# Banded attention inside a chunked delta rule: one masking pass, normalising on ScalarE, and the transpose of the weights behind the chunk's products

## The chip, the cores and the metric

The kernel runs on one core of a Trainium2 chip. The time is device microseconds of one execution. The core has TensorE (PE; its weight loads are shown as PEld), VectorE (DVE), ScalarE (ACT), GpSimd (POOL) and SyncE (SP), each with its own instruction queue, executed in order. They wait for each other only by semaphores.

## The reference

Two layers follow one another in float32 on 512 tokens of width 1024. The first mixes a gated delta rule (4 heads of 128, in chunks) with a dilated attention (8 heads of 64), adds a gated feed-forward network, and the second block holds a gated recurrence of 16 heads and a Fourier mixer. The change touches the dilated attention only:

```python
DIL_PATTERNS = ((128, 1), (512, 4), (2048, 16))
# each (window, dilation) branch attends to t, t-d, ..., t-window
s = einsum(q * Dh**-0.5, k); s = where(valid, s, -inf); m = max(s)
p = exp(s - m); den = sum(p); num = p @ v
# the three branches are merged by exp(m_i - m_all)
out = num_tot / den_tot
```

A key that several branches see counts as often as branches see it. So the three branches together are one softmax over keys 0 to t in which the exponential of each key is multiplied by a count from 0 to 3.

## The kernel before

**The stage.** After the input projections (tiles 0 to 27) come four chunks c = 0 to 3 of 128 tokens of the delta rule. In each, the inverse of a triangular 128 x 128 matrix per head is built up in six levels l = 1 to 6, all four heads side by side in one 512 wide operation. A level is a chain over three engines:

- TensorE: T = xx by mask product (L663, into bank 3), semaphore T.
- ScalarE: copies it to `tt` (L1101), semaphore Te.
- TensorE: XA (L673, bank 4; not in level 6) and XX (L676, bank 5).
- VectorE: subtracts them from `xx` (L1504) and `xt` (L1506). T of the next level needs `xx` and the next mask product (L1498).

Ahead of the levels is the chunk's head: VectorE forms decay differences (L1462, L1464), ScalarE takes exponentials (L1092 to L1094, semaphore eex), VectorE forms `ee` (L1470), `lt`, `at_`, the first `xt` (L1481), after which TensorE transposes it (L649). Behind the levels (step 7) TensorE forms two products (L682, L684), ScalarE copies both (L1105, L1106, semaphore uwe), TensorE forms the product with the state (L690), VectorE subtracts it (L1512), and TensorE forms output and state update (L696 to L701).

**The attention.** Its 32 blocks n (head n // 4, query block n % 4, (n % 4 + 1) * 128 keys) are woven into these steps, one per step, n = 8c + l with l = 0 to 7. Each block goes through:

- `scores(n)` on TensorE (L581, bank 0);
- `front(n)` on VectorE: scale and mask (L1420), maximum (L1423), its negative (L1425);
- `weights(n)` on ScalarE: exponential in place in `sm` (L1065);
- `back(n)` on VectorE: times the counts, with their sum (L1433, an instruction and a read of its accumulator), reciprocal (L1436), normalise (L1438, semaphore p_ready);
- `turn(n)` on TensorE: transposes the weights into bank 1 (L593), one per 128 keys;
- `place(n)` on ScalarE: copies them to `pT` (L1072);
- per head, `weigh(h)` on TensorE: weights by values (L602, bank 2); per pair of heads `pair_high` (ScalarE, L1084) and `pair_low` (VectorE, L1442) take the result out.

`sm` and `pr` have two buffers, banks 0, 1 and 2 one each.

**Order.** All queues are written out by hand in the program's order; no planner is involved. In step n VectorE does back(n-1), front(n), then the level's work. ScalarE copies T, then place(n-1), then weights(n). `attention_tail(n)` on TensorE is weigh of the head before, where n % 4 is 1, then turn(n-1); in a level it stands between T and the wait for Te. `scores(n+1)` follows XX. In ScalarE's `attention_tail(n)`, pair_high comes first for n = 9, 17, 25.

**Beside it.** In the same steps GpSimd multiplies streamed modulation weights (L424, L428, L432, two buffers in `mod`), and TensorE adds them up (`modulation`, L453) behind T, up to 1.3 sums per step. SyncE loads these weights.

Of the kernel before, what the change touches and what calls it, by code (L numbers as in the profile page):

```python
# [18 lines left out]
ALU = mybir.AluOpType  # L19
ACT = mybir.ActivationFunctionType  # L20
AX = mybir.AxisListType

P = 128
# [135 lines left out]
def build(nc, d, out, upto=99, debug=None):  # L159
# [4 lines left out]
    with ctx:  # L164
        sems = {}

        def S(name):
            if name not in sems:
                sems[name] = ctx.enter_context(nc.semaphore("s_" + name))
            return sems[name]  # L170
# [268 lines left out]
        def _(pe):  # L439
# [136 lines left out]
            def scores(n):  # L576
                h, i = n // 4, n % 4
                o = 64 * (h % 2)
                if n:
                    pe.wait_ge(S("sm_ready"), n)  # L580
                pe.matmul(bank[0][:, 0:(i + 1) * P], bqkv[o:o + 64, h // 2, i * P:(i + 1) * P],  # L581
                          bqkv[o:o + 64, 4 + h // 2, 0:(i + 1) * P], start=True, stop=True).then_inc(S("s_done"), 1)
# [30 lines left out]
            def attention_tail(n):  # L613
                if n >= 1:
                    if n % 4 == 1 and n > 1:
                        weigh(n // 4 - 1)
                    turn(n - 1)
# [3 lines left out]
            for c in range(TT):  # L621
                tok = slice(c * P, (c + 1) * P)
                n = 8 * c
                pe.wait_ge(S("ug"), c + 1)
                for h in range(4):
                    mm = pe.matmul(bank[3][:, h * P:(h + 1) * P], ones[:], G["ug"][:, h, :], start=True, stop=True)
                mm.then_inc(S("gr"), 1)
                if c:
                    pe.wait_ge(S("o_ev"), c)
                    pe.wait_ge(S("st_upd"), c)  # L630
                else:
                    pe.wait_ge(S("l2_rs"), 8)
                    pe.wait_ge(S("l2_done"), 8)
                for h in range(4):
                    pe.matmul(bank[4][:, h * P:(h + 1) * P], qkv[:, 4 + h, tok], qkv[:, 4 + h, tok], start=True, stop=True)
                for h in range(4):
                    pe.matmul(bank[5][:, h * P:(h + 1) * P], qkv[:, 4 + h, tok], qkv[:, h, tok], start=True, stop=True)
                for h in range(4):
                    mm = pe.transpose(bank[6][:, h * P:(h + 1) * P], qkv[:, 8 + h, tok], ident[:])
                mm.then_inc(S("kk"), 1)  # L640
                attention_tail(n)

                pe.wait_ge(S("eex"), c + 1)
                for h in range(4):
                    mm = pe.transpose(bank[3][:, h * P:(h + 1) * P], qkv[:, 4 + h, tok], ident[:])
                mm.then_inc(S("vk"), 1)
                pe.wait_ge(S("x1"), c + 1)
                for h in range(4):
                    mm = pe.transpose(bank[4][:, h * P:(h + 1) * P], G["xt"][:, h, :], ident[:])  # L649
                mm.then_inc(S("x1T"), 1)  # L650
                scores(n + 1)
                modulation(n)
                for l in range(1, 7):
                    q = 6 * c + l
                    n = 8 * c + l
                    pe.wait_ge(S("m_rdy"), q)
                    if l == 1:
                        pe.wait_ge(S("x1e"), c + 1)
                        pe.wait_ge(S("gkv"), c + 1)
                    else:  # L660
                        pe.wait_ge(S("xx_upd"), 5 * c + l - 1)
                    for h in range(4):
                        mm = pe.matmul(bank[3][:, h * P:(h + 1) * P], G["m%d" % (l % 2)][:, h, :], G["xx"][:, h, :],  # L663
                                       start=True, stop=True)
                    mm.then_inc(S("T"), 1)
                    modulation(n)
                    attention_tail(n)
                    pe.wait_ge(S("Te"), q)
                    if l > 1:
                        pe.wait_ge(S("x_upd"), q - 1)  # L670
                    if l < 6:
                        for h in range(4):
                            mm = pe.matmul(bank[4][:, h * P:(h + 1) * P], G["xt"][:, h, :], G["tt"][:, h, :], start=True, stop=True)  # L673
                        mm.then_inc(S("XA"), 1)
                    for h in range(4):
                        mm = pe.matmul(bank[5][:, h * P:(h + 1) * P], G["tt"][:, h, :], G["xt"][:, h, :], start=True, stop=True)  # L676
                    mm.then_inc(S("XX"), 1)
                    scores(n + 1)
                n = 8 * c + 7
                pe.wait_ge(S("x_upd"), 6 * c + 6)  # L680
                for h in range(4):
                    pe.matmul(bank[6][:, h * P:(h + 1) * P], G["xt"][:, h, :], G["vtok"][:, h, :], start=True, stop=True)  # L682
                for h in range(4):
                    mm = pe.matmul(bank[5][:, h * P:(h + 1) * P], G["gk"][:, h, :], G["xt"][:, h, :], start=True, stop=True)  # L684
                mm.then_inc(S("uw"), 1)
                attention_tail(n)
                pe.wait_ge(S("uwe"), c + 1)
                if c:
                    for h in range(4):
                        mm = pe.matmul(bank[3][:, h * P:(h + 1) * P], G["wkT"][:, h, :], G["st"][:, h, :], start=True, stop=True)  # L690
                    mm.then_inc(S("PS"), 1)
                pe.wait_ge(S("u"), c + 1)
                for h in range(4):
                    o = bank[4][:, h * P:(h + 1) * P]
                    if c:
                        pe.matmul(o, G["st"][:, h, :], G["qdec"][:, h, :], start=True, stop=False)  # L696
                    mm = pe.matmul(o, G["u"][:, h, :], G["at_"][:, h, :], start=(c == 0), stop=True)
                mm.then_inc(S("o"), 1)
                if c < TT - 1:
                    for h in range(4):  # L700
                        mm = pe.matmul(bank[5][:, h * P:(h + 1) * P], G["kend"][:, h, :], G["u"][:, h, :], start=True, stop=True)  # L701
                    mm.then_inc(S("ds"), 1)
                if c < TT - 1:
                    scores(n + 1)
                modulation(n)
# [210 lines left out]
        def _(act):  # L916
# [144 lines left out]

            def weights(n):
                w = (n % 4 + 1) * P
                act.wait_ge(S("nmx_ready"), n + 1)
                do(A.activation(sm[:, n % 2, 0:w], sm[:, n % 2, 0:w], ACT.Exp, bias=nmx[:, n:n + 1]), "pexp")  # L1065

            def place(n):
                h, i = n // 4, n % 4
# [6 lines left out]
            def attention_tail(n):  # L1075
                if n > 8 and n % 8 == 1:
                    pair_high(n // 8 - 1)
                if n:
                    place(n - 1)

            def pair_high(hp):
# [208 lines left out]
        def _(dve):  # L1290
# [123 lines left out]
            def front(n):  # L1414

                w = (n % 4 + 1) * P
                dve.wait_ge(S("s_done"), n + 1)
                if n >= 2:
                    dve.wait_ge(S("p_ready"), n - 1)
                do(X.scalar_tensor_tensor(sm[:, n % 2, 0:w], bank[0][:, 0:w], 0.125, dneg[:, T - w:T],  # L1420
                                          ALU.mult, ALU.add), "sm_ready")
                do.settle()
                do(X.tensor_reduce(mx[:, n:n + 1], sm[:, n % 2, 0:w], AX.X, ALU.max))  # L1423
                do.settle()
                do(X.tensor_scalar(nmx[:, n:n + 1], mx[:, n:n + 1], -1.0, None, ALU.mult), "nmx_ready")  # L1425

            def back(n):

                w = (n % 4 + 1) * P
                dve.wait_ge(S("pexp"), n + 1)  # L1430
                if n >= 2:
                    dve.wait_ge(S("pT_done"), n - 1)
                do(X.tensor_tensor_reduce(pr[:, n % 2, 0:w], sm[:, n % 2, 0:w], dcnt[:, T - w:T], 1.0, 0.0, ALU.mult, ALU.add,  # L1433
                                          den[:, n:n + 1]))
                do.settle()
                do(X.reciprocal(rden[:, n:n + 1], den[:, n:n + 1]))  # L1436
                do.settle()
                do(X.tensor_scalar(pr[:, n % 2, 0:w], pr[:, n % 2, 0:w], rden[:, n:n + 1], None, ALU.mult), "p_ready")  # L1438

            def pair_low(hp):  # L1440
                dve.wait_ge(S("ob_hi"), hp + 1)
# [2 lines left out]
            def attention_tail(n):  # L1444
                if n:
                    back(n - 1)
                if n > 8 and n % 8 == 2:
                    pair_low(n // 8 - 1)
# [375 lines left out]
```

## Time and profile before

| | us |
|---|---|
| median of three runs | 2395.82 (2393.82 to 2396.49) |
| the profiled execution, its own time | 2398.15 |
| its span, first to last instruction | 2396.4 |
| TensorE busy (share) | 2229.8 (93%) |
| VectorE busy | 1456.6 (61%) |
| ScalarE busy | 708.6 (30%) |
| GpSimd busy | 284.4 (12%) |
| mean granted TensorE clock | 0.958 of full speed |

Busy times are sums over the whole span, so they hide that stages differ: in the stretch of the four chunks (215 to 462 us) TensorE is busy for 201.69 of 247 us, VectorE for 185.06, GpSimd for 156.42, ScalarE for 58.84, with a granted clock of 0.88. In the timelines an instruction's start and its duration stand in microseconds; where an engine had been idle before it, brackets say how long and what ended the wait. Durations of TensorE products overlap, so distances between starts tell more than durations. The granted clock of a stretch is a mean: 1.00 is 2.4 GHz throughout, 0.50 would be 1.2 GHz throughout.

### The profile page before, as it was taken

To read this page: it belongs to the slowest core of one execution; us is meant where nothing else is said; L and a number is where in the kernel's file an instruction comes from. 1 tells how busy PE (TensorE), PEld (TensorE's weight loads), DVE (VectorE), ACT (ScalarE), POOL (GpSimd) and SP (SyncE) were. 2 spreads that over 40 slices of the span, in tenths; PEclk is the share of its full clock that TensorE was granted. 3 is DMA by queue.
4 is the path that set the end of the run, shared out by engine and by line. 5 is a ranking of instruction groups with operands and counts; after the bars stand their busy time and mean duration, and the time that the engine had idled before them with its cause. 6 is when DMAs were issued, how large, how long until landed. Compare 5 with 4: busy or idle time off the path is not lost.

```text
span 2396.4 us, 27171 instructions
## 1 busy us (share of the span) xinstructions
PE 2229.8 (93%) x10851; PEld 1781.4 (74%) x10851; DVE 1456.6 (61%) x2253; ACT 708.6 (30%) x1111; POOL 284.4 (12%) x196
## 2 busy tenths in 40 slices
PE   6998888789999997999999999999998898999998
PEld 4876666567888885788887877787886486888886
DVE  5634678638758583577777777777777624333332
ACT  4363222434324334222222222222221223332332
POOL 0011766423233120000000000000000000000000
PEclk9998888999999998999999999999999599999999
DMA  4331111233434332111111111111111022223221
GB/s 142 97 83 36 44 45 53 80 106 107 122 114 136 110 117 77 53 45 52 46 44 48 50 45 53 45 44 53 45 45 44 0 79 88 67 71 88 62 62 44
DMA packets 311134, 164.31 MB, mean 69 GB/s; under 512 B 6268, under 2 KB 308194, under 8 KB 311010
## 3 DMA queue, kind: packets, MB, share of 16 engines
q1 hardware_dynamic: 311010, 162.59, 23.2%
q8 instruction: 87, 1.43, 0.2%
q14 instruction: 37, 0.30, 0.0%
HBM read 160.47 MB, written 2.10 MB: 68 GB/s over the span
## 4 chain that ended last, share of the span: by engine, by line
PE 73%; DVE 18%; issue 4%; ACT 3%; POOL 0%; SPq 0%; DMA 0%; ACTq 0%; DVEq 0%; POOLq 0%
PE bank L470 16%; PE bank L472 16%; PE bank L471 16%; DVE KC L1673 3%; DVE MT L1695 3%; DVE QC L1675 2%; DVE QQ L1680 2%; PE bank L815 2%; PE bank L505 2%; PE bank L489 1%; PE bank L487 1%; PE bank L488 1%; PE bank L887 1%; PE bank L851 1%; PE bank L876 1%
## 5 line engine op out<-in xcount | busy, mean ns | idle before, releaser
L1307 DVE TENSOR_TENSOR wl<-stage,wh 128x1024 fp32r<-128x1024 f32 (+1 forms) x248 | 310.7, 1254 | 670.8 <-ACT wh L929 670.7
L470 PE MATMUL bank<-hh,wh 128*128 128x512 f32 x1536 | 642.5, 418 | 32.6 <-DVE hl L1325 17.7
L472 PE MATMUL bank<-hh,wl 128*128 128x512 f32 x1536 | 606.5, 395 | 0.0
L471 PE MATMUL bank<-hl,wh 128*128 128x512 f32 x1536 | 605.6, 394 | 0.0
L929 ACT ACTIVATE wh<-stage 128x1024 fp32r<-128x1024 f32 (+1 forms) x248 | 260.1, 1050 | 1034.1 <-PE bank L472 613.1
L470 PEld LDWEIGHTS bank<-hh,wh 128*128 128x128 f32 x1536 | 292.5, 190 | 110.2 <-issue 40.8
L472 PEld LDWEIGHTS bank<-hh,wl 128*128 128x128 f32 x1536 | 292.1, 190 | 63.9
L471 PEld LDWEIGHTS bank<-hl,wh 128*128 128x128 f32 x1536 | 293.6, 191 | 59.0 <-issue 5.7
L470 PE MATMUL bank<-gh,wh 128*128 128x512 f32 x432 | 179.0, 414 | 10.9 <-DVE gl L1536 6.6
L424 POOL TENSOR_TENSOR mprod<-stage,gs 128x1024 f32<-128x1024 f32 x64 | 130.8, 2043 | 463.7 <-DMA stage<-in_ada_w 458.8
L471 PE MATMUL bank<-gl,wh 128*128 128x512 f32 x432 | 170.0, 393 | 0.0
L472 PE MATMUL bank<-gh,wl 128*128 128x512 f32 x432 | 169.9, 393 | 0.0
L794 PE MATMUL bank<-QC,KC 128*128 128x128 f32 x1024 | 141.2, 283 | 7.5 <-DVE MT L1695 7.5
L794 PEld LDWEIGHTS bank<-QC,KC 128*128 128x128 f32 x1024 | 135.7, 199 | 14.9 <-issue 9.0
L487 PE MATMUL bank<-ch,wh 128*128 128x256 f32 x384 | 112.4, 293 | 0.0
L488 PE MATMUL bank<-cl,wh 128*128 128x256 f32 x384 | 108.7, 283 | 0.0
L489 PE MATMUL bank<-ch,wl 128*128 128x256 f32 x384 | 108.7, 283 | 0.0
L470 PEld LDWEIGHTS bank<-gh,wh 128*128 128x128 f32 x432 | 82.0, 190 | 33.5 <-DVE gl L1536 7.0
L1673 DVE TENSOR_TENSOR KC<-KK,QQ 128x512 f32<-128x512 f32 x144 | 101.0, 702 | 6.2 <-PE bank L794 5.2
L1675 DVE TENSOR_TENSOR QC<-qs,PP 128x512 f32<-128x512 f32 x144 | 100.7, 700 | 0.0
L428 POOL TENSOR_TENSOR mprod<-mprod 128x512 f32<-128x512 f32 x64 | 99.7, 1558 | 5.0
L1688 DVE TENSOR_TENSOR PP<-PP 128x512 f32<-128x512 f32 x144 | 97.7, 679 | 0.6
(295 smaller groups left out, 2974.1 us busy)
## 6 DMA issues: line engine op xcount, KB each, us to landing
stage<-in_hg_w_in SPq DMA_DIRECT2D x80, 512.0 KB, 3.6
stage<-in_ada_w SPq DMA_DIRECT2D x48, 512.0 KB, 3.6
stage<-in_w_up SPq DMA_DIRECT2D x44, 512.0 KB, 3.8
stage<-in_ft_w_in SPq DMA_DIRECT2D x32, 512.0 KB, 3.9
stage<-in_w_in SPq DMA_DIRECT2D x28, 512.0 KB, 3.8
stage<-in_w_down SPq DMA_DIRECT2D x16, 512.0 KB, 4.0
stage<-in_hg_w_out SPq DMA_DIRECT2D x16, 512.0 KB, 3.9
stage<-in_ft_w_out SPq DMA_DIRECT2D x16, 512.0 KB, 3.9
```

The source lines that it names most:

```text
L424: do(nc.gpsimd.tensor_tensor(mprod[:], stage[:, u["slot"], :, :], view(silc[:, v:v + 1], [[2, KT], [0, P]]), ALU.mult), f"stage_free{u['sl ...
L470: pe.matmul(bank[t % NLIN][:], wh[:, s, k, :], xh[:, k, :], start=a, stop=False)
L471: pe.matmul(bank[t % NLIN][:], wh[:, s, k, :], xl[:, k, :], start=False, stop=False)
L472: mm = pe.matmul(bank[t % NLIN][:], wl[:, s, k, :], xh[:, k, :], start=False, stop=b)
L487: pe.matmul(o, wh[:, s, k, :], ch[:, k, :], start=a, stop=False)
L488: pe.matmul(o, wh[:, s, k, :], cl[:, k, :], start=False, stop=False)
L489: mm = pe.matmul(o, wl[:, s, k, :], ch[:, k, :], start=False, stop=b)
L794: mm = pe.matmul(b[:, a * P:(a + 1) * P], kc[:, a * P:(a + 1) * P], qc[:, a * P:(a + 1) * P], start=True, stop=True)
L929: do(A.activation(wh[:, l % NSPLIT, 0:nk, :], stage[:, u["slot"], 0:nk, :], ACT.Copy), "hi_ready")
L1307: do(X.tensor_tensor(wl[:, l % NSPLIT, 0:nk, :], stage[:, u["slot"], 0:nk, :], wh[:, l % NSPLIT, 0:nk, :].bitcast(F32), ALU.subtract), f"s ...
L1673: do(X.tensor_tensor(view(kc[:, 0:1], flat), view(KK[:, 0, 0:1], sel), view(QQ[:, 0, 0:1], sel), ALU.mult))
L1675: do(X.tensor_tensor(view(qc[:, 0:1], flat), view(q[:, 0:1], flat), view(PP[:, 0, 0:1], [[2 * n, nb], [n - T, 2], [1, n]], T), ALU.mult), ...
```

## The change

Mask, scale and maximum become one VectorE instruction with an accumulator: it adds the mask to the unscaled scores, multiplies by -0.125 and takes the minimum, which is the negative of the maximum. `sm` holds the negated scaled scores, and the exponential has scale -1. Normalising moves from VectorE's L1438 to a ScalarE copy with a scale per partition, placed ahead of place(n-1). The reciprocal now signals `rden_ready`. In levels 1 to 6, TensorE's `attention_tail(n)` moves from between T and the wait for Te to behind XX, ahead of scores(n+1). Steps 0 and 7 keep TensorE's order.

```diff
@@ TensorE, levels 1 to 6
                     mm.then_inc(S("T"), 1)
                     modulation(n)
-                    attention_tail(n)
                     pe.wait_ge(S("Te"), q)
...
                     mm.then_inc(S("XX"), 1)
+                    attention_tail(n)
                     scores(n + 1)
@@ ScalarE
             def weights(n):
                 w = (n % 4 + 1) * P
-                act.wait_ge(S("nmx_ready"), n + 1)
-                do(A.activation(sm[:, n % 2, 0:w], sm[:, n % 2, 0:w], ACT.Exp, bias=nmx[:, n:n + 1]), "pexp")
+                act.wait_ge(S("sm_ready"), n + 1)
+                do(A.activation(sm[:, n % 2, 0:w], sm[:, n % 2, 0:w], ACT.Exp, scale=-1.0, bias=nmx[:, n:n + 1]), "pexp")
+
+            def normalise(n):
+                w = (n % 4 + 1) * P
+                act.wait_ge(S("rden_ready"), n + 1)
+                do(A.activation(pr[:, n % 2, 0:w], pr[:, n % 2, 0:w], ACT.Copy, scale=rden[:, n:n + 1]), "p_ready")
...
                 if n > 8 and n % 8 == 1:
                     pair_high(n // 8 - 1)
                 if n:
+                    normalise(n - 1)
                     place(n - 1)
@@ VectorE, front(n)
                 if n >= 2:
-                    dve.wait_ge(S("p_ready"), n - 1)
-                do(X.scalar_tensor_tensor(sm[:, n % 2, 0:w], bank[0][:, 0:w], 0.125, dneg[:, T - w:T],
-                                          ALU.mult, ALU.add), "sm_ready")
-                do.settle()
-                do(X.tensor_reduce(mx[:, n:n + 1], sm[:, n % 2, 0:w], AX.X, ALU.max))
-                do.settle()
-                do(X.tensor_scalar(nmx[:, n:n + 1], mx[:, n:n + 1], -1.0, None, ALU.mult), "nmx_ready")
+                    dve.wait_ge(S("rden_ready"), n - 1)
+
+                do(X.tensor_tensor_reduce(sm[:, n % 2, 0:w], bank[0][:, 0:w], dneg[:, T - w:T], -0.125, 3e38, ALU.add, ALU.min,
+                                          nmx[:, n:n + 1]), "sm_ready")
@@ VectorE, back(n)
                 do.settle()
-                do(X.reciprocal(rden[:, n:n + 1], den[:, n:n + 1]))
-                do.settle()
-                do(X.tensor_scalar(pr[:, n % 2, 0:w], pr[:, n % 2, 0:w], rden[:, n:n + 1], None, ALU.mult), "p_ready")
+                do(X.reciprocal(rden[:, n:n + 1], den[:, n:n + 1]), "rden_ready")
```

## Rows read from the trace of the kernel before

**Rows 1.** The page's part 4: the last chain by engine.

```profile
PE 73%; DVE 18%; issue 4%; ACT 3%; POOL 0%; SPq 0%; DMA 0%; ACTq 0%; DVEq 0%; POOLq 0%
```

**Rows 2.** Windows: stretch, length, busy by engine, clock; level 1, then levels 2-6.

```profile
284.84:295.94 11.10, 11.10 (x43) 7.63 (x44) 4.13 (x12) 1.76 (x4) 7.77 (x6) 0.62 0.16 47
...
233.00:262.79 29.79, 27.16 (x168) 21.95 (x167) 21.87 (x49) 7.53 (x15) 23.22 (x16) 0.89 0.15 43
295.94:325.02 29.08, 26.09 (x167) 20.08 (x166) 22.48 (x50) 7.76 (x15) 24.63 (x19) 0.94 0.19 55
359.34:386.59 27.25, 24.50 (x168) 19.51 (x167) 24.58 (x50) 7.75 (x15) 24.86 (x18) 1.00 0.20 59
422.92:452.64 29.72, 26.27 (x171) 21.28 (x170) 26.46 (x50) 7.72 (x15) 21.10 (x15) 0.94 0.33 98
```

**Rows 3.** Groups by shape, 215 to 462 us: busy us, mean ns, idle before.

```profile
L1433 DVE CUSTOM_DVE_ANT_0 pr<-sm,dcnt 128x512 f32<-128x512 f32 x8 | 7.9, 988 | 0.0
L1065 ACT ACTIVATE sm<-sm,gs 128x512 f32<-128x512 f32 x8 | 5.8, 723 | 1.1 <-DVE gs L1425 1.0
L1420 DVE SCALAR_TENSOR_TENSOR sm<-bank,dneg 128x512 f32<-128x512 f32 x8 | 5.4, 680 | 0.0
L1065 ACT ACTIVATE sm<-sm,gs 128x384 f32<-128x384 f32 x8 | 4.9, 615 | 3.1 <-DVE gs L1425 3.0
L1433 DVE DVE_READ_ACCUMULATOR2_ANT gs<- 128x1 f32 x32 | 2.5, 78 | 0.0
```

**Rows 4.** Timeline of VectorE, head of the third chunk: start, duration.

```profile
341.89 0.17 DVE L1436 RECIPROCAL gs<-gs 128x1 f32<-128x1 f32 x1
...
343.18 0.28 DVE L1420 SCALAR_TENSOR_TENSOR sm<-bank,dneg 128x128 f32<-128x128 f32 x1
...
343.89 1.13 DVE L1470 SCALAR_TENSOR_TENSOR g_ee<-g_ee,gs,cst 128x128 f32<-128x128 f32 x4
```

**Rows 5.** Timeline of TensorE and ScalarE in levels 4 to 6, second chunk.

```profile
308.69 1.06 PE L673 MATMUL bank<-g_tt,g_xt 128*128 128x128 f32 x8
309.58 1.06 PE L676 MATMUL bank<-g_xt,g_tt 128*128 128x128 f32 x8
...
320.12 0.91 PE L581 MATMUL bank<-bqkv 64*128 64x384 f32 x2
320.96 1.16 PE L663 MATMUL bank<-g_xx,g_m 128*128 128x128 f32 x8
322.16 0.60 ACT L1101 ACTIVATE g_tt<-bank 128x512 f32<-128x512 f32 x1 [3.04 <-PE bank L663]
322.71 0.44 PE L593 MATMUL bank<-ident,pr 128*128 128x128 f32 x2 [0.59 <-DVE pr L1438]
322.99 1.06 PE L676 MATMUL bank<-g_xt,g_tt 128*128 128x128 f32 x8
323.97 1.12 PE L581 MATMUL bank<-bqkv 64*128 64x512 f32 x2
325.02 1.16 PE L682 MATMUL bank<-g_vtok,g_xt 128*128 128x128 f32 x8
```

**Rows 6.** Timeline of ScalarE: the pair copy in level 1 of the second chunk.

```profile
292.91 0.60 ACT L1084 ACTIVATE gh<-bank 128x512 fp32r<-128x512 f32 x1 [5.36 <-PE bank L602]
```

**Rows 7.** Timeline of TensorE: second chunk's state product, and the stage's end.

```profile
328.25 1.16 PE L690 MATMUL bank<-g_st,g_wkT 128*128 128x128 f32 x8 [0.68 <-ACT g_wkT L1106]
...
459.76 0.60 PE L593 MATMUL bank<-ident,pr 128*128 128x128 f32 x4
461.10 2.37 PE L602 MATMUL bank<-pT,bqkv 128*64 128x512 f32 x8 [0.74 <-ACT pT L1072]
```

**Rows 8.** Timelines of TensorE and GpSimd: modulation sums, chunks 1, 3 and 4.

```profile
245.96 1.01 PE L453 MATMUL bank<-ones,mod 128*128 128x1 f32 x4 [1.53 <-POOL mod L432]
...
366.00 1.20 PE L453 MATMUL bank<-ones,mod 128*128 128x1 f32 x8
...
440.75 0.72 POOL L432 TENSOR_TENSOR mod<-mprod 128x256 f32<-128x256 f32 x1
```

## The prediction, made before the changed kernel was run

> **What bounds the kernel now.** I read the page's parts 1 and 4 first, then the windows of the stage that the diff touches, then the timelines of single levels. Over the whole span the chain that ended last is 73% TensorE and 18% VectorE [rows 1]; most of that TensorE share is dense projections the diff never enters. The diff lives between 215 and 462 us: four chunks of the gated delta rule, with 32 attention blocks (n = 0 to 31, eight per chunk, key width 128 to 512) woven in, so at most about a tenth of the time can move. Inside it I need to know, level by level, which wait ends last.
>
> Levels 2 to 6 of the four chunks last 29.79, 29.08, 27.25 and 29.72 us, with VectorE busy 22 to 26 us of each and TensorE 24 to 27 [rows 2]. Neither is full: they take turns. Call T the products at L663, XA those at L673, XX those at L676. T ends, ScalarE copies it (0.60 us), and XX or XA may start: 320.96 to 322.76, so 1.83 us from T's start with the hop. In this row block's turn (L593) was queued ahead and held XX to 322.99, 0.59 us of it TensorE waiting for VectorE's normalised weights [rows 5]. That is the wait the change is aimed at. In others T itself waited for VectorE's update of xx, which sits behind back, front and the next mask product on VectorE.
>
> **What goes.** Per block VectorE loses L1438, L1423 and L1425, and L1420 becomes a two-instruction reduction (the form of L1433: a main pass and an accumulator read of 0.08 us) [rows 3]. The new pass with a PSUM source is not in the trace. Below: 0.68 us at width 512, what L1420 takes; above: 0.99 us, the mean of L1433, whose two SBUF sources are sometimes stretched [rows 3]. I take 0.68, because one source stays in PSUM as in L1420. That removes about 1 to 1.4 us of VectorE per block, some 35 us in all, but only the part that ends a wait counts.
>
> (1) Chunk heads. Here VectorE alone is the path: back(8c-1) and front(8c) stand between the decay differences and L1470. In the third chunk the reciprocal ends at 342.06 and L1470 starts at 343.89. With front(128) alone between them (0.28 + 0.08) it starts at 342.44: 1.45 us less [rows 4]. The fourth chunk repeats this. In the second the normalise was short, I count 0.9. The first has no back and waits for ScalarE's exponentials anyway: 0. Sum -3.8 us. After L1470 everything hangs on VectorE, so nothing takes this back at once.
>
> (2) Levels 2 to 6. With VectorE lighter I rebuild a level from TensorE's own order: T to XA 1.83; XA to XX 0.90; XX to the next product 0.98; scores 0.84 for three key blocks and 1.05 for four, so 0.21 per block and 0.42, 0.63 for one and two; turn 0.28 for two blocks, 0.14 per block [rows 5]; the weighted values (L602) 2.3 [rows 7]. Turn now lies behind XX and thus in series. Level 2: 3.71 + 0.28 + 1.05 = 5.04. Level 3: 3.71 + 0.42 + 0.42 = 4.55. Level 4: 3.71 + 0.56 + 0.63 = 4.90. Level 5: 3.71 + 2.3 + 0.14 + 0.84 = 6.99. Level 6, without XA: 1.83 + 0.98 + 0.28 + 1.05 = 4.14. Together 25.6 us, 1.6 to 4.2 below the windows, 13.4 us over four chunks. That is the best end of this term.
> But two things in those windows are not VectorE's. One is GpSimd: TensorE executes modulation sums behind T, and waited 1.53 us for one in the first chunk (level 4); in the third the sums of level 3 ended at 367.20 [rows 8], 0.85 us later than the rebuilt level would want XA. In the fourth the second sum of level 5 is ready at 441.47; with 0.4 us of its products XA starts at 441.9, and the rebuilt level would have reached it at 422.92 + 1.03 (below) + 14.49 + 1.83 = 440.3, so 1.6 us wait. The second chunk has a wait like the first's, of about 0.9. The other is the clock: a granted 0.89, 0.94, 1.00, 0.94 [rows 2] means that 22%, 12%, 0 and 12% of the windows ran at 1.2 GHz, and the products lost 3.3, 1.7, 0 and 1.8 us by it. I keep both, since the idle spots that caused it (GpSimd waits) stay. New windows: 25.6 + 1.5 + 3.3 = 30.4, 25.6 + 0.9 + 1.7 = 28.2, 25.6 + 0.85 = 26.5, 25.6 + 1.6 + 1.8 = 29.0. Against the old: +0.6, -0.9, -0.8, -0.7: sum -1.8 us.
>
> **What is added: waits of turn for ScalarE.** A turn now needs ScalarE's normalise, and ScalarE works in order. In the middle levels this is free: the reciprocal is done before ScalarE has finished copying T, normalise (0.4 to 0.7 us, priced by the exponentials from SBUF, L1065, [rows 3]) ends before XX does. Not free in four places.
> (3) Level 1 of chunks 2 to 4. ScalarE first runs the pair copy (L1084), which waits for the weighted values (L602) that TensorE now executes directly before turn. So turn waits from the end of L602 for the copy and for normalise: 0.60, overlapped to 0.50, plus 0.39 (0.72 less 0.11 per block, by the two widths in [rows 3]) and hops, where before the turn followed at once [rows 6]: 1.03 each, +3.1. Queued behind turn are scores and T of level 2. In the third chunk the level-1 wait for the copy of T was hidden by L602, and the sums of that step are executed ahead of T: +0.75, T's 1.83 less its own products.
> (4) Step 7. Turn(8c+6) stood in the shadow of ScalarE's two copies, and the state product L690 started as they ended [rows 7]. Now normalise comes behind these copies, and L690 behind turn: 0.61 + 0.05 + 0.42, less the overlap of ScalarE starts, 0.87 each, three times; in the first chunk, where VectorE's wait is shortened too, 0.55. +3.2. Bounds: 0 if normalise could slip ahead (it can't, in order), 4.4 without overlap.
> (5) The end. Turn(31) ran at 459.76, and L602 at 461.10 [rows 7]. Now: o ends, ScalarE copies it, normalises 512 wide (0.72), turn, placing: 1.4 beyond the delay of (4). +1.4.
> (6) VectorE's back(n) now waits for an exponential that sits behind turn and placing. From XX's end: turn and placing 1.0, exponential 0.7, back 1.35, front 0.4, mask product 1.1, update 0.6: 5.2 us, against 5.6 to the next but one T. Covered; where L1433 or L1498 is stretched it slips. I take +0.5, bound 7 (rival C).
>
> **Sum:** -3.8 - 1.8 + 3.1 + 0.75 + 3.2 + 1.4 + 0.5 = +3.3 us. The profiled execution took 2398.15 us (span 2396.4, 1.75 around it), 2.3 above the median of the three shown; the sum is a difference and is put on that median. On the median: 2395.8 + 3.3 = 2399.1 us. A change below 0.2%, 4.8 us, could hardly be told from none; this is one of those.
>
> **Rivals.** A, faster: the clock. In level 1 of the second chunk the granted clock is 0.62 [rows 2], after TensorE stood still waiting for L1481; 0.38 x 11.10 = 4.2 us lost there, and levels 2 to 6 lose 6.8 in all. The stand-still in the heads of chunks 3 and 4 shrinks by the 1.45 us of (1). If TensorE keeps 2.4 GHz through these heads and GpSimd, less disturbed by VectorE, brings its sums earlier, 9 us come back: 2390. For it: VectorE has fewer SBUF passes. Against: the second chunk, the coldest, is helped least, and GpSimd's chain is its own.
> B, slower: the same clock the other way. After L602 in level 1, (3) opens a TensorE gap of 1 us, right after a cold stretch, and each level has 0.6 us open while T is copied, that turn used to fill. If TensorE falls to 1.2 GHz there, level 2 (5.04, of which 4.4 are products) gains some 3 us in three chunks: +9, so 2408; it decides from the point where the gap is answered by a clock below 1.
> The Trainium skill (TensorE: Matmul & The Clock Gate, "What's actually happening") says the gate's level follows how busy TensorE has recently been, idle being throttled. The trace agrees with the direction, by the 0.62 above; it would make both A and B possible and says not which.
> C, slower: VectorE is late. If L1433 (mean 0.99 at 512 [rows 3]) and the mask product are both stretched in levels 3 and 4, update comes up to 0.9 late in eight levels: +7, less what is in (6): 2405. Against: the removed pass L1438 was a victim of the same stretching.
> D: the relief counts in full, the 13.4 of (2) instead of 1.8: 2387.5. Against: the sums from GpSimd are needed and not faster.
>
> **Chances.** Forecast and near it (2395 to 2403) 0.52; A 0.14; D 0.04; B 0.18; C 0.12. The range of 8 in 10 reaches into A and B: 2390 to 2405.5. The likeliest case's own is 2395 to 2403. Slower by over 0.2% takes B, C and the upper edge of the forecast: 0.33. Faster: most of A and D, 0.18. Same: 0.49.
>
> **What would show it.** Right: L1470 1.4 us earlier behind the reciprocal in the third and fourth chunk; XX or XA 1.83 us behind every T without sums; turn waiting on ScalarE, about 1 us, behind L602 in level 1 and before L690; the new pass 0.68 us at 512. Wrong: a new pass near 1 us; T waiting for xx in levels 3 and 4 (C); a granted clock in levels 2 to 6 off its 0.89 to 1.00 (A up, B down); or anything outside 215 to 490 us moving by more than the shift, which I exclude.

## The result, and the profile after

The changed kernel takes 2400.62 us (median of 19 runs, 2398.76 to 2406.58), the kernel before 2395.77 us on the same chips: ratio 1.0021, 95% interval 1.0014 to 1.0028. That is 4.9 us slower; the interval, 3.4 to 6.7 us, leaves out no change. In two experiments below, one pass only and L602 in front, one execution took far longer (4461 and 2504 us); it is in the medians and not in the ratios. The forecast was 2399.1 us, +3.3.

The profiled execution has a span of 2398.8 us, only 2.4 above the one of before. That understates the change. The first transpose of the stage (L649) starts at 218.37 us instead of 221.81, though the head before it takes as long (7.58 us, before 7.57) and nothing ahead of that head was changed; in the other profiles it starts anywhere from 218.2 to 222.0. So I measure from there to the first column sum behind the stage (L520): 245.89 us before, 252.48 after, and 250.27 in a second profile of the same changed kernel. One profile of this stretch is uncertain by a few microseconds, as shown below; whether a kernel is faster or slower is read from the ratios.

First the page of the changed kernel, parts 1 and 4, against [rows 1].

```profile
PE 2233.2 (93%) x10851; PEld 1785.0 (74%) x10851; DVE 1425.2 (59%) x2189; ACT 723.6 (30%) x1143; POOL 283.7 (12%) x196
...
PE 74%; DVE 17%; issue 4%; ACT 4%; POOL 1%; SPq 0%; DMA 0%; DVEq 0%; ACTq 0%; POOLq 0%
```

VectorE works 31 us less, ScalarE 15 us more, and the kernel is slower: most of the 31 us did not shorten the time. Groups by shape in the stage, 212 to 475 us (busy us, mean ns, idle before), against [rows 3]:

```profile
L1427 DVE CUSTOM_DVE_ANT_0 sm<-bank,dneg 128x512 f32<-128x512 f32 x8 | 5.5, 692 | 0.3 <-DVE gs L1439 0.3
L1427 DVE DVE_READ_ACCUMULATOR2_ANT gs<- 128x1 f32 x32 | 2.7, 83 | 0.0
L1070 ACT ACTIVATE pr<-pr,gs 128x512 f32<-128x512 f32 x8 | 5.7, 719 | 1.1 <-DVE gs L1439 1.1
L1070 ACT ACTIVATE pr<-pr,gs 128x384 f32<-128x384 f32 x8 | 4.9, 614 | 0.0
```

The new reduction from PSUM takes 0.69 us at width 512 (0.68 was taken), its accumulator read 0.08, normalise on ScalarE 0.72 and 0.61 (as taken). The prices of single instructions were right; what decides is where they lie. Windows of levels 2 to 6 in chunks 1 to 4, then level 1 of chunk 3, against [rows 2]; behind the five busy times stands the granted clock:

```profile
230.55:260.52 29.97, 27.72 (x168) 22.27 (x167) 17.21 (x39) 9.72 (x20) 21.05 (x16) 0.88 0.13 36
293.82:321.31 27.49, 24.75 (x167) 19.54 (x166) 18.60 (x40) 9.67 (x20) 23.11 (x17) 1.00 0.20 58
358.47:385.27 26.80, 24.75 (x167) 19.53 (x166) 19.14 (x40) 9.78 (x20) 23.44 (x17) 1.00 0.21 59
423.38:451.86 28.48, 26.61 (x172) 21.60 (x171) 18.83 (x40) 9.84 (x20) 19.58 (x15) 0.94 0.32 93
...
347.69:358.47 10.78, 9.12 (x36) 6.68 (x36) 2.66 (x9) 2.15 (x5) 8.13 (x6) 0.71 0.17 50
```

TensorE's timeline in chunk 3, level 1 and on (start, duration, idle before with its releaser), and the step 7 that follows:

```profile
347.69 2.06 PE L663 MATMUL bank<-g_xx,g_m 128*128 128x128 f32 x8
350.43 2.07 PE L672 MATMUL bank<-g_tt,g_xt 128*128 128x128 f32 x8 [0.69 <-ACT g_tt L1107]
352.30 1.80 PE L675 MATMUL bank<-g_xt,g_tt 128*128 128x128 f32 x8
354.03 2.37 PE L602 MATMUL bank<-pT,bqkv 128*64 128x512 f32 x8
357.38 0.33 PE L593 MATMUL bank<-ident,pr 128*128 128x128 f32 x1 [0.97 <-ACT pr L1070]
...
389.00 0.55 PE L593 MATMUL bank<-ident,pr 128*128 128x128 f32 x3 [1.68 <-ACT pr L1070]
389.38 1.06 PE L690 MATMUL bank<-g_st,g_wkT 128*128 128x128 f32 x8
391.29 0.73 PE L696 MATMUL bank<-g_qdec,g_st 128*128 128x128 f32 x2 [0.85 <-DVE g_u L1513]
391.81 0.64 PE L697 MATMUL bank<-g_at__85,g_u 128*128 128x128 f32 x2
...
461.22 0.66 PE L593 MATMUL bank<-ident,pr 128*128 128x128 f32 x4 [1.30 <-ACT pr L1070]
462.56 4.06 PE L602 MATMUL bank<-pT,bqkv 128*64 128x512 f32 x8 [0.69 <-ACT pT L1077]
```

All three new waits of turn for ScalarE's normalise are there: 0.97 behind L602, 1.68 in step 7, 1.30 at the end. The output products behind such a wait can run at 1.2 GHz: in chunk 3 it is 0.43 us from one pair of products to the next (391.81 to 392.24), against 0.22 in the same place of the kernel before. The last L602 takes 4.06 instead of 2.37 us [rows 7]. The head of chunk 3 on VectorE, against [rows 4]:

```profile
338.97 0.16 DVE L1439 RECIPROCAL gs<-gs 128x1 f32<-128x1 f32 x1
339.09 0.29 DVE L1427 CUSTOM_DVE_ANT_0 sm<-bank,dneg 128x128 f32<-128x128 f32 x1
339.31 0.08 DVE L1427 DVE_READ_ACCUMULATOR2_ANT gs<- 128x1 f32 x1
339.31 1.69 DVE L1471 SCALAR_TENSOR_TENSOR g_ee<-g_ee,gs,cst 128x128 f32<-128x128 f32 x4
```

From the reciprocal's end to L1471 (before: L1470) it is 0.18 us, before it was 1.83: 1.65 us gone. But four instructions that took 1.13 now take 1.69, and they start while GpSimd still works (its L428 runs from 338.46 to 340.06; before, it ended at 342.97, ahead of L1470). Net 1.09.

The whole stage, cut at the same instructions in every profile. Level 1 is T(1) to T(2); levels 2 to 6 from T(2) to the first product of step 7; head from the first product of a chunk (L626) to L649; each cell chunks 1, 2, 3, 4 (the head of chunk 1 lies ahead; the last step 7 runs to L520):

| us | level 1 | levels 2 to 6 | step 7 to next chunk | heads 2, 3, 4 | stage |
|---|---|---|---|---|---|
| before | 7.92, 11.10, 7.78, 9.68 | 29.79, 29.08, 27.25, 29.72 | 7.77, 12.31, 12.30, 15.06 | 11.02, 10.46, 10.47 | 245.89 |
| after | 8.92, 11.26, 10.78, 10.75 | 29.97, 27.49, 26.80, 28.48 | 8.15, 13.09, 14.72, 18.99 | 10.62, 9.37, 9.38 | 252.48 |
| after, second profile | 7.91, 12.73, 11.77, 12.05 | 28.74, 27.49, 26.80, 26.88 | 8.14, 13.08, 13.09, 18.99 | 10.62, 9.37, 9.37 | 250.27 |

Heads give 2.6 us, levels 2 to 6 give 3.1 (5.9 in the second profile), L649 to T(1), not in the table, 0.5 (0.9); level 1 costs 5.2 (8.0), step 7 and the end 7.5 (5.9). Over the whole stage the granted clock was 0.87 before, 0.85 after and 0.88 in the second profile. That second profile is 4.4 us longer than the one of before at no lower a clock, so the clock alone is not the loss.

### The profile page after: what moved, and what is told of

It reads as the page before. It is cut to its first block, busy times and chain, and to the rows that moved or that the text cites. A ratio compares the mean times of both kernels' runs of the same rounds, so it can differ in the third digit from the quotient of the medians.

```text
span 2398.8 us, 27139 instructions
## 1 busy us (share of the span) xinstructions
PE 2233.2 (93%) x10851; PEld 1785.0 (74%) x10851; DVE 1425.2 (59%) x2189; ACT 723.6 (30%) x1143; POOL 283.7 (12%) x196
## 4 chain that ended last, share of the span: by engine, by line
PE 74%; DVE 17%; issue 4%; ACT 4%; POOL 1%; SPq 0%; DMA 0%; DVEq 0%; ACTq 0%; POOLq 0%
PE bank L470 16%; PE bank L472 16%; PE bank L471 16%; DVE KC L1674 3%; DVE MT L1696 3%; DVE QC L1676 2%; DVE QQ L1681 2%; PE bank L815 2%; PE bank L505 2%; PE bank L489 1%; PE bank L487 1%; PE bank L488 1%; PE bank L794 1%; PE bank L887 1%; PE bank L851 1%
## 5 line engine op out<-in xcount | busy, mean ns | idle before, releaser
L428 POOL TENSOR_TENSOR mprod<-mprod 128x512 f32<-128x512 f32 x64 | 98.2, 1534 | 5.0
```

## The experiments

Theory: the lighter VectorE is a gain, and the loss is ScalarE's order, which puts normalise behind work that turn did not wait for. Rivals: the loss is turn's place in series behind XX; or VectorE's relief is worth nothing; or it is all the clock. The ratios are to the kernel before, and a difference called "by the ratios" is a difference of ratios times 2396 us.

| kernel | median us | ratio, 95% interval | stage in its profile |
|---|---|---|---|
| one pass only | 2392.26 | 0.9981 (0.9971 to 0.9990) | 244.18 |
| one pass only, again | 2392.44 | 0.9988 (0.9977 to 0.9999) | 247.33 |
| changed, normalise early | 2393.24 | 0.9984 (0.9976 to 0.9993) | 239.36 |
| changed, turn in front | 2398.43 | 1.0011 (1.0002 to 1.0020) | 250.16 |
| before, turn behind | 2400.45 | 1.0016 (1.0008 to 1.0025) | 248.19 |
| early, L602 in front | 2390.65 | 0.9971 (0.9960 to 0.9983) | 240.05 |
| the same again | 2390.30 | 0.9977 (0.9968 to 0.9986) | 239.97 |
| the same, normalise on VectorE | 2393.98 | 0.9990 (0.9981 to 0.9999) | 245.11 |
| changed, fillers in the gaps | 2397.12 | 1.0008 (0.9999 to 1.0016) | 248.43 |
| changed, normalise before pair copy | 2399.22 | 1.0009 (0.9999 to 1.0018) | 249.89 |
| changed, again | 2400.64 | 1.0016 (1.0007 to 1.0025) | 250.27 |

**One pass only.** The kernel before with `front` and the exponential's scale of the change; the rest stays.

```diff
-  scalar_tensor_tensor; tensor_reduce max; tensor_scalar -1
+  do(X.tensor_tensor_reduce(sm[...], bank[0][...], dneg[...], -0.125, 3e38, ALU.add, ALU.min, nmx[:, n:n + 1]), "sm_ready")
```

> Only the one-pass mask, scale and maximum; normalise stays on VectorE, turn stays ahead of the wait for the copy of T. Theory (the change loses by turn's new waits for ScalarE, and its VectorE part is a gain): 3 us less than before, from 0.36 us in three or four chunk heads and from levels 3 and 4, where T waited 0.3 to 1.2 us for VectorE: ratio 0.9985. Rival (VectorE's relief is worth nothing, all is taken back by GpSimd sums and the clock): ratio 1.000. Rival (the PSUM-source reduction is itself slow): above 1.000.

Measured 0.9981 and, when repeated, 0.9988: 4.5 and 2.9 us faster by the ratios, about as expected. VectorE's part is a gain by itself; the rival that GpSimd and the clock take it all back falls. The heads of chunks 3 and 4 give 0.5 us each (9.97 and 9.96); where the rest lies these profiles do not settle, since their stages, 244.18 and 247.33 us, lie on both sides of the 245.89 of before.

**Normalise early.** ScalarE's order alone is changed in the changed kernel.

```diff
+                if n and n % 8 != 7 and n != 32:
+                    normalise(n - 1)
                 if n > 8 and n % 8 == 1:
                     pair_high(n // 8 - 1)
                 if n:
-                    normalise(n - 1)
                     place(n - 1)
...
+                normalise(8 * c + 6)
                 act.wait_ge(S("uw"), c + 1)
...
+                if c == TT - 1:
+                    normalise(31)
                 act.wait_ge(S("o"), c + 1)
```

> The changed kernel, but ScalarE normalises before the pair copy in level 1, before it waits for the two products of step 7, and before it waits for the last output. Theory: the waits of turn of 0.98, 1.68 and 1.30 us shrink to near 0, 7 us less than the changed kernel, 2 to 3 below before: ratio 0.999; turn starts right behind L602 in level 1, and L690 starts as ScalarE's copies end. Rival (the loss is turn's place in series behind XX): stays at 1.002. Rival (the loss is a clock that fell in the gaps): between the two, depending on which gaps vanish.

Measured 0.9984: 8.9 us less than the changed kernel by the ratios, 7.7 by the ratio of its repeat, 7.4 by the medians. In its profile, chunk 2, turn waits 0.30 us before step 7's state product instead of 1.68, and the product again starts as ScalarE's copies end:

```profile
319.99 0.55 PE L593 MATMUL bank<-ident,pr 128*128 128x128 f32 x3 [0.30 <-ACT pr L1070]
320.96 1.16 PE L690 MATMUL bank<-g_st,g_wkT 128*128 128x128 f32 x8 [0.42 <-ACT g_wkT L1114]
```

Step 7 is back at 7.61, 12.41, 12.30 and 15.06 us, the values of before. Level 1 falls from 41.7 to 39.9 us in all, levels 2 to 6 from 112.7 to 109.0. This is the decisive run: normalise earlier in ScalarE's queue at eight places, no work less, is the difference between slower and faster. It also rules out turn's place behind XX as the whole loss, since turn stands there here too. Some of the gain is clock: the slow last L602 and the slow outputs of chunk 3 are gone with the waits. And the kernel is no faster than the one pass alone.

**Normalise before the pair copy only.**

```diff
+                if n:
+                    normalise(n - 1)
                 if n > 8 and n % 8 == 1:
                     pair_high(n // 8 - 1)
                 if n:
-                    normalise(n - 1)
                     place(n - 1)
```

> The changed kernel with a single swap: in level 1 ScalarE normalises before the pair copy. Theory: three waits of 0.98 us go, 2.9 us less than the changed kernel: ratio 1.0008; the waits before L690 (1.68) and at the end (1.30) stay. Rival (these waits are covered by something else): 1.002.

Measured 1.0009, level 1 of chunks 2 to 4 at 11.65, 9.78 and 10.77 us, against 12.73, 11.77 and 12.05 in the second profile of the changed kernel: 1.1 to 2.0 each; against the first profile (11.26, 10.78, 10.75) it is 0.4 more, 1.0 less and the same. The three waits of 0.98 are gone, those of 1.68 and 1.30 stand. In this profile the last step 7 takes 20.53 us: the outputs of chunk 4 and the last L602 both ran at 1.2 GHz. By the ratios the kernel is 1.7 to 2.9 us below the changed one, of 2.9 expected, but the intervals overlap.

**Turn in front, normalise on ScalarE.**

```diff
                     modulation(n)
+                    attention_tail(n)
                     pe.wait_ge(S("Te"), q)
...
-                    attention_tail(n)
                     scores(n + 1)
```

> The changed kernel with turn back ahead of the wait for the copy of T, normalise still on ScalarE. Theory: turn now waits for ScalarE's normalise behind its copy of T in every level, so XA starts 0.6 us and the turn itself later: 0.6 us in 24 levels less what levels 5 and 1 give back, +8 to +13 us against the changed kernel: ratio 1.006. Rival (turn in series behind XX is the loss): faster than the changed kernel, 1.000 or below.

Measured 1.0011. The expected loss of 8 to 13 us against the changed kernel did not come; it is even or slightly less slow. The waits are there as told, in chunk 2, level 3 (the last line is the stage's last L602):

```profile
299.27 1.16 PE L663 MATMUL bank<-g_xx,g_m 128*128 128x128 f32 x8
301.62 0.55 PE L593 MATMUL bank<-ident,pr 128*128 128x128 f32 x3 [1.19 <-ACT pr L1070]
...
304.29 1.16 PE L663 MATMUL bank<-g_xx,g_m 128*128 128x128 f32 x8
...
461.90 2.37 PE L602 MATMUL bank<-pT,bqkv 128*64 128x512 f32 x8 [0.69 <-ACT pT L1077]
```

The level takes 5.02 us, the same level of the changed kernel 5.41 (298.92 to 304.33), of which T waits 0.78 for VectorE's xx. My sum for the expectation was wrong: T to turn is 2.35, only 0.5 above the 1.83 that XA waits anyway; turn itself is in series in both orders; and with turn behind XX, VectorE's back starts later. So the change's move of turn, within the changed kernel, gains nothing; by the ratios it costs 1.2 to 2.4 us, not separated by the intervals. The waits of 1.68 and 1.30 are in this profile too. The outputs of chunk 3 are again slow behind them (step 7 14.61 us), while the last L602 runs at full clock (2.37).

**Before, with only turn moved.** The same move of `attention_tail(n)` as in the change, nothing else.

> The kernel before with only turn moved behind XX. Theory: VectorE still carries mask, maximum and normalise, and its back now also waits for an exponential that sits behind turn and placing: from XX's end 1.8 + 2.1 + 1.6 + 1.1 + 0.6 = 7.2 us to the xx update, against 5.6 that TensorE needs, so T waits about 1 us or more in levels 3 and 4 and in part in level 2: +8 us, ratio 1.0035 or more. Rival (turn's place is the whole loss of the change): 1.002. Rival (turn behind XX is free or a gain by itself): below 1.000.

Measured 1.0016, 3.9 us, half of what was expected. That is also what the rival "turn's place is the whole loss" foretold. The early normalise rules it out as the whole, but the move costs something in the kernel before. The one pass with an early normalise and turn still in front was not run, so what the move is worth in the best order stays open. In this profile T does wait for xx (0.94, 0.41, 0.23, 0.41, 1.08 and 1.75 us, 4.8 in all), and yet levels 2 to 6 sum to 113.9 us against 115.8 before, because turn's own waits for VectorE are gone. The loss is in level 1: 11.09, 10.61 and 10.26 in chunks 2 to 4. In chunk 3 this is 2.83 us more, with no wait of turn at all in it. The part that moves with turn here is L602. The profile of this run, level 1 of chunk 3:

```profile
345.09 2.08 PE L663 MATMUL bank<-g_xx,g_m 128*128 128x128 f32 x8 [0.55 <-DVE g_m L1489]
347.86 2.07 PE L672 MATMUL bank<-g_tt,g_xt 128*128 128x128 f32 x8 [0.69 <-ACT g_tt L1101]
349.72 1.91 PE L675 MATMUL bank<-g_xt,g_tt 128*128 128x128 f32 x8
351.57 3.11 PE L602 MATMUL bank<-pT,bqkv 128*64 128x512 f32 x8
354.60 0.33 PE L593 MATMUL bank<-ident,pr 128*128 128x128 f32 x1
```

0.69 is the uncovered copy; the other 2 us are that XA and XX run at 1.2 GHz, and part of L602. Before, they ran at full clock behind L602 (1.06 us each).

**L602 back in front.** On top of the early normalise.

```diff
                     modulation(n)
+                    if n % 4 == 1 and n > 1:
+                        weigh(n // 4 - 1)
                     pe.wait_ge(S("Te"), q)
...
                 if n >= 1:
-                    if n % 4 == 1 and n > 1:
-                        weigh(n // 4 - 1)
                     turn(n - 1)
```

> As e2_early_norm, but the weighted values (L602) go back ahead of the wait for the copy of T, and only turn stays behind XX. Theory: L602 again hides the 0.69 us that TensorE idles for the copy in level 5 of the first chunk and level 1 of the third, and the pair copy no longer has turn behind it: 1.5 to 2 us less than e2_early_norm, ratio 0.9977. Rival (the GpSimd sums and the clock take this back): the same as e2_early_norm, 0.9984.

Measured 0.9971, and 0.9977 when repeated: the fastest of all, some 6 us below before and 11 below the changed kernel. Against the early normalise alone the intervals overlap; the gain of 1.5 to 3 us there is as expected but not separated by them. Level 1 of chunk 3 shows what L602's place does and does not do:

```profile
345.41 4.31 PE L602 MATMUL bank<-pT,bqkv 128*64 128x512 f32 x8
349.66 1.16 PE L672 MATMUL bank<-g_tt,g_xt 128*128 128x128 f32 x8
```

Now L602 covers the copy, but runs at 1.2 GHz itself (4.31 us, 4.28 in the repeat; 2.98 before). The level takes 9.18 and 9.15 us, against 9.72 with L602 behind XX and 7.78 before. So its place is worth 0.5 us here; the remaining 1.4 us is a clock that rose later behind T, and no run isolates why. In chunk 4, level 5, TensorE now reaches GpSimd's sum early and waits 2.80 us for it (2.83 in the repeat, 1.97 in the early normalise, none in the changed kernel): there GpSimd takes back part of the gain.

> f1_weigh_front once more, to stand beside g1 and g3 on the same chip. Ratio 0.997; heads 9.37 us in chunks 3 and 4, step 7 of the third chunk 12.3 us in every profile, if those are order and not chance.

Heads 9.39 and 9.37 us and step 7 of chunk 3 at 12.30 came out as told.

**The same with normalise on VectorE, and one pass again.**

```diff
-  do(X.reciprocal(rden[...], den[...]), "rden_ready")
+  do(X.reciprocal(...)); do.settle(); do(X.tensor_scalar(pr[...], pr[...], rden[...], None, ALU.mult), "p_ready")
```

> f1_weigh_front with normalise back on VectorE: one-pass mask and maximum, L602 ahead of the wait for the copy of T, turn behind XX. It tells what ScalarE's normalise is worth once its order is mended. Theory: heads lose 0.6 us in chunks 2 to 4 (1.8 us), and in levels 3 and 4 VectorE's update comes up to 0.5 us later: 2 to 3 us more than f1_weigh_front, ratio 0.998. Rival (normalise on ScalarE is worth nothing in any order): equal to f1_weigh_front, 0.997.

> e1_onepass once more, on the same chip. Ratio 0.998. Theory: f1's order is 2 us faster than it (heads 9.37 against 9.96 us in chunks 3 and 4, 0.4 in chunk 2, and levels without turn's waits for VectorE). Rival: no difference, then the one-pass reduction alone is the whole useful part of the change.

Measured 0.9990 for normalise on VectorE and 0.9988 for the one pass, against 0.9977. By the medians, normalise on ScalarE is worth 3.7 us once its order is mended, by the ratios 3.1, as the theory had it; but the interval of 0.9977 (0.9968 to 0.9986) still overlaps both others, so this size is likely and not settled. The heads show where: 11.02, 9.98 and 9.96 us against 10.62, 9.39 and 9.37. Most of the rest is one stretch, levels 2 to 6 of chunk 4 (33.04 against 30.48).

**Fillers.** The changed kernel with products into the free bank 3 ahead of turn: 4, 7 and 5 in the three kinds of gap.

```diff
+            def filler(k):
+                for i in range(k): h = i % 4; pe.matmul(bank[3][h], G["tt"][h], G["tt"][h], start=True, stop=True)
...
+                    if n > 8 and n % 8 == 1:
+                        filler(4)
+                    if n % 8 == 7:
+                        filler(7)
+                    if n == 32:
+                        filler(5)
                     turn(n - 1)
```

> The changed kernel with extra products into a free bank in the three gaps ahead of turn (4 in level 1 of chunks 2 to 4, 7 in each step 7, 5 at the end; 0.22 us each at full clock), so that TensorE does not idle there while turn waits as long. Theory (the gaps also lower the clock behind them: 1.55 us in the outputs of the third chunk and 1.7 us in the last L602): those two stretches run at full clock and 2 to 3 us come back: ratio 1.001. Rival (only the waits themselves cost): 1.002, or above if the fillers are longer than the gaps.

Measured 1.0008, 3.5 us less than the changed kernel by the medians though turn starts no earlier and work was added. The intervals of the ratios overlap, by which it is 1.9 to 3.1 us; but nine of its eleven executions lie below 2399.2 us and ten of the eleven of the changed kernel's repeat above. In its profile the last L602 is at full clock:

```profile
460.80 0.66 PE L593 MATMUL bank<-ident,pr 128*128 128x128 f32 x4 [0.18 <-ACT pr L1081]
462.14 2.37 PE L602 MATMUL bank<-pT,bqkv 128*64 128x512 f32 x8 [0.69 <-ACT pT L1088]
```

The last step 7 is 17.31 us, 1.68 less than in both profiles of the changed kernel. But the profile of turn in front has 17.31 too, without a filler, so this L602 alone does not show what the fillers did. The faster median does speak for it that part of the loss is clock that the new gaps cost; in which places is not shown.

**The changed kernel again.**

> The changed kernel itself once more, for a second profile beside the first. Theory: the waits of turn (0.98, 1.68, 1.30) repeat to 0.05 us, since they are order; the places where the granted clock falls do not all repeat, so single stretches differ by 1 to 3 us. Rival: the clock's places repeat too, then they belong to the change as much as the waits. Ratio 1.002.

The waits repeat: 0.98, 0.98 and 0.97; 1.68 four times; 1.30. The clock repeats in part: the last L602 takes 4.06 us again, but the outputs of chunk 3 ran at full clock this time (13.09 instead of 14.72), and level 1 cost 2.8 us more. So these places are partly chance, but not free of the waits. Of the four profiles that have the waits of 1.68 and 1.30 and no fillers (changed twice, turn in front, normalise before pair copy), three have slow outputs in one chunk and three a slow last L602. Of the eight profiles without these waits, none has either in chunks 2 to 4.

## Why the prediction was right

It said +3.3 us, with a chance of 0.49 for a change within 0.2% and 0.33 for slower by more. Measured was +4.9, just over that line: the direction is right and the time lies inside the likeliest case's own range (2395 to 2403). What carried it is the mechanism of terms (3) to (5), turn waiting for a normalise that stands late in ScalarE's queue, which the early normalise confirms. That the sum comes so near is in part luck: the terms below are off by 1 to 4 us each, with opposite signs.

- (1) Heads, -3.8 expected, -2.6 measured, in all profiles alike. The freed path was right (1.65 us behind the reciprocal, 1.45 expected). What I left out: L1470's four instructions, which started just after GpSimd's work before, now start into it and take 0.56 longer in chunks 3 and 4, 0.72 in chunk 2 (3.87 for 3.15).
- (2) Levels 2 to 6, -1.8 expected, -3.1 and -5.9 measured. The rebuilt levels hold: level 2 is 5.10 us where 5.04 was expected, level 4 4.86 (4.90), XA or XX 1.84 us behind T with 0.69 idle for the copy. That GpSimd and the clock would leave little of the 13.4 us was right in the first profile (chunk 4: 28.48 against 29.0; chunk 3: 26.80 against 26.5); in the second it left nearly half. Too high were the two things that I kept from before: the waits for GpSimd's sums in the first profile were 0.88, 0.59, 0.64 and none instead of 1.5, 0.9, 0.85 and 1.6, and the windows lost 5.3 and 1.7 us by the clock instead of 6.8.
- (3) Level 1, +3.85 expected, +5.2 and +8.0 measured. Each wait is there (0.97 for 1.03, 0.69 for 0.75). Left out is the clock's share, the other 1.6 and 4.4 us: in chunk 3 the granted clock of level 1 fell from 0.79 to 0.71 and 0.65, and XA and XX ran at 1.2 GHz. The turn-behind experiment shows this without any wait of turn. L602's place is not the reason for most of it, since L602 in front ran at 1.2 GHz itself (4.31 us).
- (4) and (5) Step 7 and the end, +4.6 expected, +7.5 and +5.9 measured: 0.78 for 0.87 per chunk, 0.38 for 0.55 in the first, and at the end 2.24 to L602, for 0.87 + 1.4. On top, unexpected, 1.7 us for the slow last L602, and 1.6 for the slow outputs in the first profile.
- (6) and rival C: T of level 4 did wait for xx, 0.78 us in chunk 2 and 0.84 in chunk 4, in both profiles: more than the 0.5 in all, less than the 7.
- Rival B had the right mechanism, a clock answering the new gaps, in other places than told: not in level 2 of chunks 2 to 4, which ran at 2.4 GHz (5.10 us), but in level 1, step 7 and the end. By the differences above it cost there 4.9 and 6.1 us in the two profiles, against 9, and levels 2 to 6 got 1.5 and 5.1 of it back. Rival A did not come: in chunk 3's level 1 the clock fell. That TensorE waited only 2.1 us for GpSimd's sums, where 4.85 were counted, does not speak for it either: in chunk 4 TensorE came later than counted, and with L602 in front, where it came earlier, it waited 2.80 us. The Trainium skill (TensorE: Matmul & The Clock Gate, "What's actually happening") ties the level to recent activity, and the filler experiment agrees in direction: with TensorE kept busy in the gaps the median was 3.5 us lower.

What stays open: which of the clock's falls a given order will cause. Two profiles of one kernel differ by up to 3.2 us in the stage and 2.3 us in one stretch (both in the one pass), and by 0.1 us in L602 in front.

## What to carry to other kernels

Before moving an operation to an idle engine, write down what stands ahead of it in that engine's queue at each place where its consumer waits, boundaries of the loop first: here the normalises' waits lay in eight of 32 places, and moving those ahead of work they did not depend on was worth 7.4 to 8.9 us and turned +0.21% into -0.16%. Where a product hides a wait, moving it with its neighbour uncovers that wait: look whether the two can be moved apart (here likely worth 1.5 to 3 us, which the intervals do not settle). Try the parts of a change alone; the one-pass maximum alone was a gain of 3 to 4.5 us, while the changed kernel as a whole lost 4.9.

## What the runs showed that was not expected

Time freed on VectorE was partly taken back by GpSimd: L1470's group, from SBUF only, went from 1.13 to 1.69 us when its earlier start made it overlap GpSimd's L428; no run isolates the overlap as the cause, but all thirteen profiles agree with it. In chunks 1, 3 and 4 the group took 1.13 or 1.14 us in the 23 cases in which no GpSimd instruction ran beside it, and 1.69 or 1.70 in the 16 in which L428's last 0.75 us did. And 45 products of 0.22 us whose result nobody reads, put into TensorE's idle places, made the median of the changed kernel 3.5 us lower.
